# A hybrid attention trunk: the softmax denominators' small transfers issued by ScalarE instead of SyncE

## The chip, the cores and the metric

The kernel runs on one core of a Trainium2 chip. The metric is the device time of one execution in microseconds. Before the change it is 4072.53 us, the median of 3 runs (4071.81 to 4072.68).

## The reference

Two layers of a transformer trunk work on 1024 latent tokens and 256 context tokens of width 1024. Each layer has an input projection, four parallel mixers, an output projection and an MLP. Three of the mixers are attentions, and the kernel runs each as several heads:

```python
# A: neighbourhood attention (latents) or dense (context), 4 heads
p = jax.nn.softmax(jnp.concatenate([s_loc, s_ctx], axis=-1), axis=-1)
# B: differential attention, 4 heads with two softmaxes each
p1 = jax.nn.softmax(jnp.einsum('bqhd,bkhd->bhqk', a, k1) * scale, axis=-1)
p2 = jax.nn.softmax(jnp.einsum('bqhd,bkhd->bhqk', b, k2) * scale, axis=-1)
out = jnp.einsum('bhqk,bkhe->bqhe', p1 - lam * p2, v)
# D: banded attention with a sink logit, 4 heads
p = jax.nn.softmax(jnp.concatenate([s_loc, s_ctx, s_sink], axis=-1), axis=-1)
```

The fourth mixer is a Fourier transform over tokens and channels. Everything is float32.

## The kernel before

The kernel is written by hand, engine by engine, with semaphores. In the attention stage of each layer there are 16 heads, numbered v: 0 to 7 are the B heads (four heads, two softmaxes each), 8 to 11 the A heads, 12 to 15 the D heads. Each head has three chunks of query tokens (512, 512 and 256), and each chunk is a job. A job is made of key steps: 12, 12 and 2 for a B head, 10, 10 and 2 for an A head, 9, 9 and 2 for a D head, 376 in all for a layer. A key step is one block of 128 keys: TensorE makes the scores (`scores`, lines 2190 to 2193) in one of three PSUM banks, ScalarE takes the exponential into one of five `prob` buffers (line 1446), and two steps later TensorE multiplies by the values (`values`, line 2210). In A and D heads VectorE adds a bias or a mask to the scores first (`add_bias`, lines 1788 and 1791).

Between the key steps TensorE and VectorE make the row maxima of the next job. This is done in pieces (`piece`, lines 2162, 1757 and 1765), spread over the key steps by a planner (`SLOT_PIECES`). Two PSUM banks hold the pieces, so TensorE cannot make a piece before VectorE has reduced the one two before it. Each engine runs its own instructions in order; a wait at one of them holds all that stand behind it.

The value matrix has 64 columns of ones beside its 64 columns of values, so one half of the output holds the values' sum and the other half the softmax denominators. ScalarE copies both to `o_raw` (`take`, line 1477) two steps after a job's last key step. What follows for a head v happens during head v + 1:

1. `denominators_out` (line 1056): one row of `o_raw`, 1280 numbers, goes to DRAM (`s_den`).
2. `denominators_in` (line 1062): it comes back spread over 128 partitions (`den_c`).
3. `invert` (line 1795): VectorE takes the reciprocals in its slot at the end of the head's first job (`RECIP_AT`; step 11 in a B head, 9 in an A head, 8 in a D head). It waits there for `den_c`.
4. `reciprocals` (line 1066): SyncE stores `den_r` to DRAM (`s_rden`), waits for it, and loads it back broadcast over 64 partitions (`rden`).
5. `scale` (line 1222): GpSimd multiplies `o_raw` by `rden`.
6. For odd heads of A and D, ScalarE and VectorE split the result in two parts (`upper_pair`, line 1465; `lower_pair`, line 1812) at the steps of `PAIR_AT`: the last step of the second job and the two steps after it. SyncE stores them (`store_out`, line 1077).

All transfers of the stage are issued by SyncE, in this order for each v (lines 1093 to 1127): the loads of head v + 1 (`load_head`, gated on the start of head v), in heads 9 and 10 eight loads of bias tables (`load_bias`), then `denominators_out(v - 1)`, `load_values(v + 1)`, `denominators_in(v - 1)`, at v = 1 the first bias tables, `reciprocals(v - 1)`, at v = 8 the Fourier stage's loads, at v = 12 and 13 the transform matrices (`load_transform`), and the stores of a finished pair. ScalarE issues transfers only in the stage before (lines 1332 and 1407).

Of the kernel before, what the change touches and what calls it, by code (L numbers as in the profile page):

```python
# [23 lines left out]
P = 128  # L24
# [4 lines left out]
TOK = LAT + SEQ  # L29
# [10 lines left out]
NCH = len(CHUNKS)  # L40
# [88 lines left out]
def attention_jobs():  # L129

    jobs, v = [], 0
    for kind, heads in (("B", [(h, s) for h in range(4) for s in range(2)]), ("A", [(h, 0) for h in range(4)]),
                        ("D", [(h, 0) for h in range(4)])):
        for h, s in heads:
            for c in range(NCH):
                jobs.append((kind, h, s, c, v))
            v += 1
    return jobs
# [48 lines left out]
JOBS = attention_jobs()  # L187
NJ = len(JOBS)
# [14 lines left out]
NV = NJ // NCH  # L203
# [37 lines left out]
TAKE_AT = [STEP0[j + 1] + LAG for j in range(NJ)]  # L241
# [148 lines left out]

RECIP_AT = [STEP0[(v + 1) * NCH + 1] - 1 for v in range(NV - 1)]
assert len(set(ROW_AT)) == NJ and len(set(TAKE_AT)) == NJ
PAIR_AT = {STEP0[(v + 1) * NCH + 2] - 1 + c: (v, c) for v in PAIRS if v < NV - 1 for c in range(NCH)}
D_JOBS = [j for j in range(NJ) if JOBS[j][0] == "D"]
T_USES = [sum(1 for i in range(NT) if i % 2 == b) for b in range(2)]
# [29 lines left out]
def trunk(nc, I, O):  # L425
# [4 lines left out]
    def sem(name):  # L430
        return ctx.enter_context(nc.semaphore(name))
# [10 lines left out]
    def at(name, shape, dt, off):  # L442
        size = 4 * int(np.prod(shape[1:]))
        assert off + size <= top, (name, off + size, top)
        return nc.alloc_sbuf_tensor_at(name, shape, dt, offset=off).ap(), off + size

    def put(name, shape, dt=F32):
        ap, cur["c"] = at(name, shape, dt, cur["c"])
        cur["c"] = -(-cur["c"] // 32) * 32
        return ap  # L450
# [5 lines left out]
    for s in range(3):  # L456
        a, o = at(f"w_hi{s}", [P, 2048], F32R, W0 + s * 16384)
# [68 lines left out]
    a, o = at("w_hi3", [P, 2048], F32R, TMP2 + 8192)  # L526
# [63 lines left out]
    fc_r, o = at("fc_r", [P, FKT, 256], F32, cur["c"])  # L590
    flip, o = at("flip", [P, P], F32, o)
# [5 lines left out]
    o_raw = [put(f"o_raw{i}", [P, TOK]) for i in range(2)]  # L597
    rden = put("rden", [P, TOK])
    den_c, den_1, den_r = put("den_c", [P, TOK // P]), put("den_1", [P, TOK // P]), put("den_r", [P, TOK // P])
# [11 lines left out]
    def scratch(name, shape):  # L611
        return nc.dram_tensor(name, shape, F32).ap()
# [5 lines left out]
    s_den, s_rden = scratch("s_den", [16, TOK]), scratch("s_rden", [16, TOK])  # L618
# [43 lines left out]
    sink_p, o_mul, o_free = sem("sink_p"), sem("o_mul"), sem("o_free")  # L662
    den_out, den_in, den_rdy, rden_out, rden_in = (sem("den_out"), sem("den_in"), sem("den_rdy"), sem("rden_out"),
                                                   sem("rden_in"))
# [15 lines left out]
    def settle(e):  # L680

        e.sem_inc(seen, 1)  # L682
# [169 lines left out]
    def _(sp):  # L852
# [30 lines left out]
        for l in range(DEPTH):  # L883
# [116 lines left out]
            def load_transform(x):  # L1000
                sp.dma_start(dft_t[:, x], I["k_dft_lat"][x].rearrange("(t p) n -> p t n", p=P)).then_inc(f_in, 16)
                sp.dma_start(dft_x[:, x], I["k_dft_ctx"][x].rearrange("(t p) n -> p t n", p=P)).then_inc(f_in, 16)
# [44 lines left out]
            def load_bias(h):  # L1047

                for w, tab, sm in ((0, na_q[h % 2], bq_in[h % 2]), (1, na_k[h % 2], bk_in[h % 2])):
                    for half, c0, r, n in BIAS_PARTS[w]:  # L1050
                        sp.dma_start(tab[half * 64:half * 64 + 64, c0:c0 + n * GRID_W],
                                     s_toe[l, h, w, :, r * GRID_W:(r + n) * GRID_W]).then_inc(sm, 16)
# [3 lines left out]
            def denominators_out(v):  # L1056
                h = JOBS[v * NCH][1]
                d = 64 - 64 * (h % 2)
                sp.wait_ge(o_free, l * NJ + (v + 1) * NCH)
                sp.dma_start(s_den[v:v + 1], o_raw[v % 2][d:d + 1]).then_inc(den_out, 16)  # L1060

            def denominators_in(v):
                sp.wait_ge(den_out, l * NV * 16 + (v + 1) * 16)
                sp.dma_start(den_c, s_den[v].rearrange("(p t) -> p t", p=P)).then_inc(den_in, 16)

            def reciprocals(v):
                h = JOBS[v * NCH][1]
                o = 64 * (h % 2)
                sp.wait_ge(den_rdy, l * NV + v + 1)
                sp.dma_start(s_rden[v].rearrange("(p t) -> p t", p=P), den_r).then_inc(rden_out, 16)  # L1070
                sp.wait_ge(rden_out, l * NV * 16 + (v + 1) * 16)
                if v:
                    sp.wait_ge(o_mul, l * NV + v)
                sp.dma_start(rden[o:o + 64], bass.AP(tensor=s_rden.tensor, offset=v * TOK, ap=[[0, 64], [1, TOK]])
                             ).then_inc(rden_in, 16)
# [17 lines left out]
            for v in range(NV):  # L1093
                kind, h = JOBS[v * NCH][:2]
                if v + 1 < NV:
                    load_head(v + 1)
                if kind == "A" and 1 <= h < 3:
                    sp.wait_ge(s1_max, l * PIECES + PIECE0[v * NCH])
                    settle(sp)
                    sp.wait_ge(s2_add, l * NADD + ADD0[v * NCH])  # L1100
                    load_bias(h + 1)
                if v:
                    denominators_out(v - 1)
                if v + 1 < NV:
                    load_values(v + 1)
                if v:
                    denominators_in(v - 1)
                if v == 1:
                    sp.wait_ge(toe_in, (l + 1) * TOE_DMAS * 16)
                    sp.wait_ge(b_init, l * 4 + 4)  # L1110
                    settle(sp)
                    load_bias(0)
                    load_bias(1)
                if v:
                    reciprocals(v - 1)
                if kind == "A" and h == 0:
                    load_fourier()
                if v * NCH == FIRST_D:
                    sp.wait_ge(s1_max, l * PIECES + PIECE0[FIRST_D])
                    settle(sp)  # L1120
                    sp.wait_ge(s2_add, l * NADD + ADD0[FIRST_D])
                    settle(sp)
                if kind == "D" and h < 2:
                    load_transform(h)
                if v - 1 in PAIRS:
                    for cc in range(NCH):
                        store_out(JOBS[(v - 1) * NCH][0], JOBS[(v - 1) * NCH][1] // 2, cc)
# [189 lines left out]
    def _(act):  # L1317
# [36 lines left out]
        for l in range(DEPTH):  # L1354
# [70 lines left out]
            def max_row(j):  # L1425

                kind, _, _, c, v = JOBS[j]
                c0, n = CHUNKS[c]
                r, dst = (96, q1[v % 2]) if kind == "B" else (64, q2[v % 2])
                act.wait_ge(m_rowp, l * NJ + j + 1)  # L1430
                act.activation(dst[r:r + 1, c0:c0 + n], bank[r:r + 1, 7, :n], ACT.Copy, scale=-1.0).then_inc(m_rdy, 1)  # L1431
# [33 lines left out]
            def upper_pair(v, c):  # L1465
                c0, n = CHUNKS[c]
                act.wait_ge(o_mul, l * NV + v + 1)
                upper_out(pair_index(v, c), o_ad[:, c0:c0 + n], n)

            def take(j):  # L1470

                c0, n = CHUNKS[JOBS[j][3]]
                v = JOBS[j][4]
                act.wait_ge(pv_done, l * STEPS + STEP0[j + 1])
                if v >= 2:
                    act.wait_ge(o_mul, l * NV + v - 1)
                act.activation(o_raw[v % 2][:, c0:c0 + n], bank[:, 5 + j % 2, :n], ACT.Copy).then_inc(o_free, 1)

            max_row(0)
            for s in range(STEPS + LAG + 1):  # L1480
                if s < STEPS:
                    j, i = STEP_JOB[s]
                    exponentials(j, i)
                if s in ROW_AT:
                    max_row(ROW_AT.index(s))
                if s < STEPS and i == 0 and JOBS[j][0] == "D":
                    sink_row(j)
                if s in TAKE_AT:
                    take(TAKE_AT.index(s))
                if s in PAIR_AT:  # L1490
                    upper_pair(*PAIR_AT[s])

# [109 lines left out]
    def _(dve):  # L1602
# [33 lines left out]
        for l in range(DEPTH):  # L1636
# [175 lines left out]
            def lower_pair(v, c):  # L1812
                c0, n = CHUNKS[c]
                lower_out(pair_index(v, c), o_ad[:, c0:c0 + n], n)
# [5 lines left out]
            for s in range(STEPS + LAG + 1):  # L1820
# [7 lines left out]
                if s in RECIP_AT:  # L1828
                    invert(RECIP_AT.index(s))
                if s - 1 in PAIR_AT:  # L1830
                    lower_pair(*PAIR_AT[s - 1])

# [575 lines left out]
```

## Time and profile before

| what | value |
|---|---|
| median of 3 runs | 4072.53 us |
| profiled execution, its own time | 4076.61 us |
| its span, first to last instruction | 4074.9 us |
| mean granted TensorE clock | 0.977 |
| TensorE busy | 3845.0 us (94%) |
| VectorE busy | 2099.4 us (52%) |
| ScalarE busy | 916.3 us (22%) |
| GpSimd busy | 558.4 us (14%) |

The engine names in the rows are PE (TensorE matmul), PEld (its weight load), DVE (VectorE), ACT (ScalarE), POOL (GpSimd) and SPq and ACTq (the issuing of transfers by SyncE and ScalarE). An engine is busy from the start to the end of an instruction; the brackets at the end of a line tell how long it stood idle before, and what ended the wait. A transfer has two times: that of its issue, which holds the issuing engine, and that to its landing, which is told apart.

### The profile page before, as it was taken

Reading aid. Unit: us, or ns where it says so; the run is one execution under the profiler, and the core shown is the slowest. Engines: PE = TensorE matmul, PEld = TensorE weight load, DVE = VectorE, ACT = ScalarE, POOL = GpSimd, SP = SyncE. Lnnn points to the kernel's source line nnn. Section 1 sums busy time; section 2 is a strip of 40 time slices with the busy share of each in tenths; the row PEclk is TensorE's granted clock in tenths of the full one; section 3 lists DMA queues with packets and bytes.
Section 4 is the critical chain, followed back from the end, with each engine's and each line's share of the span. In section 5 each row is a group of like instructions: output and inputs, shape, how many; then the busy total and the mean of one; then the engine's idle time right before and its main releaser. Section 6 shows DMA issues by size and latency. Waiting matters only on the chain. (4 is left out here: it accounts for less than half of the span.)

```text
span 4074.9 us, 47294 instructions
## 1 busy us (share of the span) xinstructions
PE 3845.0 (94%) x18444; PEld 2989.6 (73%) x18444; DVE 2099.4 (52%) x3442; ACT 916.3 (22%) x1718; POOL 558.4 (14%) x432
## 2 busy tenths in 40 slices
PE   6898999889999999999989989999999999999998
PEld 4787556565888888888868855566568888888886
DVE  5222555555476666665572245555546545454445
ACT  3111455443210000000031125544512000000002
POOL 0011011101211111111131101110022111111112
PEclk8999999999999999999999989999999999999999
DMA  6754223564122122112215433256440100110011
GB/s 228 224 186 127 65 54 80 140 144 145 43 83 63 47 73 73 54 56 73 63 51 183 137 82 83 50 125 138 106 166 32 42 32 32 42 42 32 32 42 52
DMA packets 289646, 358.53 MB, mean 88 GB/s; under 512 B 102994, under 2 KB 215508, under 8 KB 289296
## 3 DMA queue, kind: packets, MB, share of 16 engines
q1 hardware_dynamic: 269008, 350.54, 29.5%
q10 hardware_dynamic: 20416, 4.98, 0.6%
q8 instruction: 146, 2.39, 0.2%
q14 instruction: 76, 0.62, 0.1%
HBM read 288.28 MB, written 72.16 MB: 88 GB/s over the span
## 5 line engine op out<-in xcount | busy, mean ns | idle before, releaser
L2056 PE MATMUL bank<-h_hi,w_hi 128*128 128x512 f32 (+1 forms) x2496 | 905.4, 363 | 21.1 <-issue 14.7
L2057 PE MATMUL bank<-h_lo,w_hi 128*128 128x512 f32 (+1 forms) x2496 | 886.2, 355 | 0.0
L2058 PE MATMUL bank<-h_hi,w_lo 128*128 128x512 f32 (+1 forms) x2496 | 886.0, 355 | 0.0
L2210 PE MATMUL bank<-prob,vv 128*128 128x512 f32 (+3 forms) x1504 | 703.7, 549 | 0.0
L1874 DVE SCALAR_TENSOR_TENSOR xT<-bank,mods,xT 128x512 f32<-128x512 f32 (+1 forms) x816 | 536.8, 661 | 321.9 <-PE bank L2058 305.2
L2056 PE MATMUL bank<-m_hi,w_hi 128*128 128x512 f32 (+1 forms) x1536 | 569.8, 371 | 53.1 <-DVE xT L1874 51.3
L2056 PEld LDWEIGHTS bank<-h_hi,w_hi 128*128 128x128 f32 x2496 | 472.7, 189 | 103.5 <-issue 33.8
L2058 PE MATMUL bank<-m_hi,w_lo 128*128 128x512 f32 (+1 forms) x1536 | 547.0, 356 | 0.0
L2057 PE MATMUL bank<-m_lo,w_hi 128*128 128x512 f32 (+1 forms) x1536 | 546.0, 355 | 0.0
L2057 PEld LDWEIGHTS bank<-h_lo,w_hi 128*128 128x128 f32 x2496 | 472.8, 189 | 73.4 <-issue 7.7
L2058 PEld LDWEIGHTS bank<-h_hi,w_lo 128*128 128x128 f32 x2496 | 472.6, 189 | 66.7
L1757 DVE TENSOR_REDUCE mp<-bank 128x1 f32<-128x512 f32 (+1 forms) x576 | 378.0, 660 | 274.1 <-PE bank L2162 273.3
L1557 ACT ACTIVATE m_r<-bank 128x512 f32<-128x512 f32 (+1 forms) x192 | 100.9, 527 | 1676.6 <-PE bank L2058 1676.6
L1446 ACT ACTIVATE prob<-bank 128x512 f32<-128x512 f32 (+1 forms) x576 | 329.0, 573 | 387.9 <-PE bank L2190 264.1
L2056 PEld LDWEIGHTS bank<-m_hi,w_hi 128*128 128x128 f32 x1536 | 289.7, 189 | 136.0 <-DVE xT L1874 87.1
L2162 PE MATMUL bank<-k,q 96*128 96x512 f32 (+4 forms) x768 | 288.4, 391 | 78.3 <-DMA sink_rows<-in_k_sink_rows 30.7
L1914 DVE TENSOR_TENSOR m_f<-m_r 128x512 f32<-128x512 f32 (+1 forms) x192 | 115.6, 603 | 461.6 <-ACT m_r L1557 461.6
L2190 PE MATMUL bank<-q,k 97*128 97x512 f32 (+1 forms) x416 | 322.5, 775 | 1.8 <-ACT q L1431 1.8
L2058 PEld LDWEIGHTS bank<-m_hi,w_lo 128*128 128x128 f32 x1536 | 290.0, 189 | 43.1
L2057 PEld LDWEIGHTS bank<-m_lo,w_hi 128*128 128x128 f32 x1536 | 290.5, 189 | 41.4 <-issue 0.9
L715 POOL TENSOR_SCALAR w_hi<-stage 128x2048 fp32r<-128x2048 f32 x90 | 173.5, 1927 | 1073.6 <-issue 537.1
L719 DVE TENSOR_TENSOR w_lo<-stage,w_hi 128x2048 fp32r<-128x2048 f32 x90 | 212.8, 2364 | 186.4 <-POOL w_hi L715 186.4
(187 smaller groups left out, 4080.7 us busy)
## 6 DMA issues: line engine op xcount, KB each, us to landing
stage<-in_w_mlp SPq DMA_DIRECT2D x64, 1024.0 KB, 5.2
nx_w<-in_w_ada SPq DMA_DIRECT2D x16, 1536.0 KB, 9.2
stage<-in_w_in SPq DMA_DIRECT2D x18, 1024.0 KB, 6.3
ada_h<-in_w_ada SPq DMA_DIRECT2D x16, 1024.0 KB, 7.9
rope_t<-in_k_rope SPq DMA_DIRECT2D x28, 512.0 KB, 4.4
k<-s_kB SPq DMA_DIRECT2D x48, 224.0 KB
k<-s_kA SPq DMA_DIRECT2D x24, 448.0 KB, 10.5
k<-s_kD SPq DMA_DIRECT2D x24, 448.0 KB, 10.7
```

What stands on the lines that cost most here:

```text
L715: pool.tensor_scalar(w_hi[slot], stage, 1.0, 0.0, ALU.mult, ALU.add).then_inc(whi_rdy, 1)
L719: dve.tensor_tensor(w_lo[slot], stage, w_hi[slot].bitcast(F32), ALU.subtract).then_inc(wlo_rdy, 1)
L1446: act.activation(prob[si % NP_RING][:, :n], src, ACT.Exp, scale=FS if kind == "B" else 1.0).then_inc(p_rdy, 1)
L1757: dve.tensor_reduce(mp[j % 2][:, t, x:x + 1], src, AX.X, ALU.max).then_inc(s1_max, 1)
L1874: dve.scalar_tensor_tensor(out=x, in0=bank[:, bk, :n], scalar=mods[l][:, gate + k, cd:cd + 1], in1=x, op0=ALU.mult, op1=ALU.add).then_inc( ...
L1914: dve.tensor_tensor(m_f[m][:, :n], m_r[m][:, :n], m_r[m][:, :n], ALU.mult).then_inc(sqr_rdy, 1)
L2056: x = pe.matmul(out, a_hi, b_hi, start=first, stop=False)
L2057: pe.matmul(out, a_hi, b_lo, start=False, stop=False)
L2058: return x, pe.matmul(out, a_lo, b_hi, start=False, stop=last)
L2162: pe.matmul(bank[:, gi % 2, :n], q1[v % 2][0:rows, q0:q0 + P], k1[v % 2][0:rows, key0:key0 + n], start=True, stop=True).then_inc(s1_full, 1)
L2190: mm = pe.matmul(out, k1[b][0:97, k], q1[b][0:97, q], start=True, stop=True)
L2210: pe.matmul(ob[:, q0:q0 + n], vv[h % 2][:, key0 // P], prob[si % NP_RING][:, :n], start=(i == 0 and kind != "D"), stop=(i == len(steps) - ...
```

## The change

The four transfers of a head's denominators leave SyncE's order and are issued by ScalarE at fixed key steps of the next head. Counted from the first step of head v + 1, the transfer out comes after step 3, the one in after step 7 (B) or 6 (A and D), the reciprocals' store two steps after VectorE's slot, and their broadcast load six (B) or five steps after it (the kind is that of head v). Only the last head of each layer keeps SyncE's versions.

```diff
+DEN_OUT_AT = {TAKE_AT[(v + 1) * NCH - 1] + 1: v for v in range(NV - 1)}
+DEN_IN_AT = {s + (4 if JOBS[v * NCH][0] == "B" else 3): v for s, v in DEN_OUT_AT.items()}
+RDEN_OUT_AT = {s + 2: v for v, s in enumerate(RECIP_AT)}
+RDEN_IN_AT = {s + 6 if JOBS[v * NCH][0] == "B" else s + 5: v for v, s in enumerate(RECIP_AT)}
...
-                if v:
-                    denominators_out(v - 1)
                 if v + 1 < NV:
                     load_values(v + 1)
-                if v:
-                    denominators_in(v - 1)
...
-                if v:
-                    reciprocals(v - 1)
...
+            def denominators_out(v):
+                d = 64 - 64 * (JOBS[v * NCH][1] % 2)
+                act.wait_ge(o_free, l * NJ + (v + 1) * NCH)
+                act.dma_start(s_den[v:v + 1], o_raw[v % 2][d:d + 1]).then_inc(den_out, 16)
+
+            def denominators_in(v):
+                act.wait_ge(den_out, l * NV * 16 + (v + 1) * 16)
+                act.dma_start(den_c, s_den[v].rearrange("(p t) -> p t", p=P)).then_inc(den_in, 16)
+
+            def reciprocals_out(v):
+                act.wait_ge(den_rdy, l * NV + v + 1)
+                act.dma_start(s_rden[v].rearrange("(p t) -> p t", p=P), den_r).then_inc(rden_out, 16)
+
+            def reciprocals_in(v):
+                o = 64 * (JOBS[v * NCH][1] % 2)
+                act.wait_ge(rden_out, l * NV * 16 + (v + 1) * 16)
+                if v:
+                    act.wait_ge(o_mul, l * NV + v)
+                act.dma_start(rden[o:o + 64], bass.AP(tensor=s_rden.tensor, offset=v * TOK, ap=[[0, 64], [1, TOK]])
+                              ).then_inc(rden_in, 16)
...
+                if s in DEN_OUT_AT:
+                    denominators_out(DEN_OUT_AT[s])
+                if s in DEN_IN_AT:
+                    denominators_in(DEN_IN_AT[s])
+                if s in RDEN_OUT_AT:
+                    reciprocals_out(RDEN_OUT_AT[s])
+                if s in RDEN_IN_AT:
+                    reciprocals_in(RDEN_IN_AT[s])
                 if s in PAIR_AT:
                     upper_pair(*PAIR_AT[s])
```

## Rows read from the trace of the kernel before

**Rows 1.** The page, part 1: busy time, share of the span and instructions.

```profile
PE 3845.0 (94%) x18444; PEld 2989.6 (73%) x18444; DVE 2099.4 (52%) x3442; ACT 916.3 (22%) x1718; POOL 558.4 (14%) x432
```

**Rows 2.** Waits, longest in total: total us, times, longest us.

```profile
DVE den_r L1801 <- DMA den_c<-s_den: 58.6, 12, 6.7
```

**Rows 3.** Stretches (heads 8, 9, 11, 13): us; PE, PEld, DVE, ACT, POOL; clock, DMA, GB/s.

```profile
692.80:723.00 30.20, 29.94 (x124) 20.11 (x124) 20.05 (x65) 14.59 (x28) 5.83 (x2) 1.00 0.69 164
723.00:762.00 39.00, 32.87 (x126) 22.09 (x125) 20.23 (x66) 14.58 (x28) 2.89 (x1) 0.91 0.54 119
...
800.00:833.00 33.00, 29.96 (x123) 20.03 (x122) 20.38 (x63) 15.63 (x31) 2.92 (x1) 1.00 0.57 137
...
863.00:896.00 33.00, 27.63 (x107) 18.47 (x106) 14.91 (x42) 13.76 (x28) 2.90 (x1) 0.90 0.68 168
```

**Rows 4.** Timeline of head 9: start us, us, what, idle before and its releaser.

```profile
723.08 0.45 SPq L1023 DMA_DIRECT2D q<-s_qA  x1
...
732.70 0.44 SPq L1060 DMA_DIRECT2D s_den<-o_raw  x1
...
733.60 4.20 SPq L1042 DMA_DIRECT2D vv<-in_cache_na_v  x1
...
741.97 0.34 SPq L1064 DMA_DIRECT2D den_c<-s_den  x1
744.52 0.22 DVE L1801 RECIPROCAL den_r<-den_c 128x10 f32<-128x10 f32 x1 [6.63 <-DMA den_c<-s_den]
...
745.30 0.80 PE L2162 MATMUL bank<-k,q 128*128 128x512 f32 x1 [5.88 <-DVE mp L1765]
```

**Rows 5.** Timeline of head 9, ScalarE's exponentials of steps 3 and 6.

```profile
728.40 0.60 ACT L1446 ACTIVATE prob<-bank 128x512 f32<-128x512 f32 x1 [0.57 <-PE bank L2193]
...
734.03 0.63 ACT L1446 ACTIVATE prob<-sb 128x512 f32<-128x512 f32 x1 [1.21 <-DVE sb L1791]
```

**Rows 6.** Timeline of heads 8, 12 and 13: inversions, a head's start, a piece.

```profile
708.13 0.22 DVE L1803 RECIPROCAL den<-den_c 128x10 f32<-128x10 f32 x1 [0.46 <-DMA den_c<-s_den]
...
833.08 0.44 SPq L1023 DMA_DIRECT2D q<-s_qD  x1
...
849.10 0.22 DVE L1801 RECIPROCAL den_r<-den_c 128x10 f32<-128x10 f32 x1 [3.04 <-DMA den_c<-s_den]
...
881.24 0.22 DVE L1801 RECIPROCAL den_r<-den_c 128x10 f32<-128x10 f32 x1 [4.76 <-DMA den_c<-s_den]
...
882.06 0.79 PE L2162 MATMUL bank<-k,q 128*128 128x512 f32 x1 [3.11 <-DVE mp L1757]
```

**Rows 7.** Two stretches, columns as in rows 3 (DMA share is next to last).

```profile
729.00:735.00 6.00, 6.00 (x26) 3.99 (x24) 4.95 (x17) 1.81 (x4) 0.00 (x0) 1.00 1.01 216
272.80:278.80 6.00, 6.00 (x52) 6.00 (x51) 0.00 (x0) 0.35 (x1) 1.45 (x1) 1.00 0.97 313
```

**Rows 8.** Line 1332 (ScalarE's queue), the one transfer issued at 213.44.

```profile
DMA to landing us min/median/max: 2.2/2.2/2.2
```

**Rows 9.** Line 1332, the one transfer issued at 272.77.

```profile
DMA to landing us min/median/max: 6.0/6.0/6.0
```

**Rows 10.** Line 1064, the loads of `den_c`, all 32.

```profile
DMA to landing us min/median/max: 1.5/2.1/2.8
```

**Rows 11.** Line 1051, the `na_q` table loads of head 9.

```profile
L1051 SPq DMA_DIRECT2D na_q<-s_toe x4: 597/597/1317, 726.9 to 729.5; - x4
...
DMA to landing us min/median/max: 9.7/10.2/10.8
```

**Rows 12.** Line 1074, the broadcast loads of `rden`, all 32.

```profile
DMA to landing us min/median/max: 3.5/3.8/4.3
```

**Rows 13.** Timeline of head 12, GpSimd's multiplication.

```profile
855.16 2.92 POOL L1234 TENSOR_TENSOR o_ad<-o_raw,rden 64x1280 f32<-64x1280 f32 x1 [26.16 <-DMA rden<-s_rden]
```

**Rows 14.** Timeline before attention, an issue of SyncE.

```profile
204.65 1.44 SPq L953 DMA_DIRECT2D cache_n<-in_cache_na_k  x1
```

**Rows 15.** Timeline before attention, an issue of ScalarE.

```profile
205.38 0.83 ACTq L1332 DMA_DIRECT2D s_toe<-in_na_rpb_rev  x1
```

## The prediction

> **What bounds the kernel now.** I read the engine totals first: TensorE is busy for 94% of the span, ScalarE for 22% [rows 1]. A change that only moves DMA issues can gain only where TensorE stands still or runs at a lower clock. Then the waits: VectorE waited 58.6 us, in 12 waits of up to 6.7 us, for `den_c`, the denominators on their way back from DRAM [rows 2]. Then busy time in stretches of one attention head each (v counts the 16 heads of a layer: 0 to 7 are B, 8 to 11 A, 12 to 15 D). Head 8 takes 30.2 us and TensorE is busy for 29.94 of them at full clock. Head 9, with the same work, takes 39.0: TensorE is busy for 32.87 us at a mean clock of 0.91. Head 13 takes 33.0 at 0.90 [rows 3]. So the reader should see some 9 us lost in one head: about 6 in idle time and 2.9 in matmuls at the lower level (1.2 against 2.4 GHz) right after it.
>
> The timeline of head 9 shows who does it [rows 4]. SyncE starts the next head's loads at 723.08, issues the tiny `s_den` store only at 732.70, behind 14 large loads, spends 4.20 us on issuing one `vv` load from 733.60, and can issue the `den_c` load only at 741.97. VectorE, whose slot for the inversion came at 737.89 (744.52 - 6.63), starts it at 744.52, and TensorE, whose next row piece needs VectorE, has stood for 5.88 us at 745.30. Head 11 has 33.0 - 29.96 = 3.0 us of idle time at full clock, against 0.3 in head 8 [rows 3]. In head 12 VectorE waits 3.04, in head 13 4.76, and TensorE then stands for 3.11 [rows 6]. So TensorE's idle time is the wait less 0.75 in A and less 1.65 in D, which makes 1.4 for head 12. In head 8 VectorE waits 0.46. The B heads do not wait at all: the 12 waits lie in heads 9 to 14 of the two layers.
>
> **The change, part by part.** Removed from SyncE: for 15 of 16 heads in each layer two waits with the transfers out and in, and the two waits around the reciprocals. Its next items then start earlier: the Fourier loads of head 8, the transform loads of heads 12 and 13. They are no nearer to their use, so I count nothing for them, except that they keep the DMA engines full while the small transfers run. Behind every later head load SyncE is held by its own gates, which stay.
>
> Added to ScalarE: four issues for each of these 30 heads. I take SyncE's 0.44 us of 732.70 for each, 1.8 a head, 53 us in all. ScalarE waited 0.57 and 1.21 us before the two steps shown [rows 5], with two steps of score banks ahead of it. An issue of 0.44 fits, so I count 0; without that cover it would be 53 us.
>
> Moved: the first transfer now leaves after key step 3. In head 9 that exponential starts at 728.40 and takes 0.60, so the transfer goes at 729.0, which is 6.0 after the head's start and 3.7 earlier than now. The second goes after step 6, 734.03 + 0.63 = 734.66, so 11.6 after the start at the earliest [rows 5]. What decides is how long a transfer takes to land on ScalarE's queue while SyncE's queue fills the DMA engines: their share was 1.01 between 729 and 735 [rows 7]. The trace of before has no such denominators, only ScalarE's table writes. One issued at 213.44 into idle engines landed in 2.2 us, one at 272.77 with a share of 0.97 in 6.0 [rows 8, 9, 7]: 3.8 more. `den_c` itself lands in 1.5 us at best [rows 10]. The bounds are therefore 1.5 (no delay) and 10.8, the slowest table load in SyncE's own queue [rows 11]. I take 1.5 + 3.8 = 5.3 for both, because the write at 272.77 is the nearest row: small pieces, same queue, full engines. Then `s_den` has landed at 6.2 + 5.3 = 11.5, just before step 6 asks, and `den_c` at 11.7 + 0.34 + 5.3 = 17.3 after the head's start. The slot comes at 14.8 in an A head (737.89 - 723.08) and at 13.0 in a D head (849.10 - 3.04 - 833.08) [rows 4, 6]: waits of 2.5 and 4.3 remain.
>
> The Trainium skill (DMA: Bandwidth & Descriptors, Queues, rings and completion order) says that each DMA engine alternates between the queues at packet granularity. By that rule a transfer of one packet would hardly be delayed and the sum would be that of the first rival; the 3.8 us above speak against taking it whole.
>
> What comes next in heads 9 and 10: the first piece after the inversion needs the bias table of the next head. Its last `na_q` load is issued at 729.5 and lands 10.2 us later, at 739.7 [rows 11], 16.6 after the head's start. That is the next wait, and it is just inside 17.3.
>
> The sum for the first layer, in TensorE time:
> - Heads 9 and 10: idle 5.88 becomes 2.5 - 0.75 = 1.75, so -4.1, and the slow matmuls go, -2.9 (32.87 - 29.94): head 11 had more idle time than that at a clock of 1.00. -7.0 each, -14.0.
> - Head 8: a wait of 0.46 becomes 2.5: +1.6.
> - Head 11: 3.0 becomes the 0.3 of head 8, -2.7; its pieces leave VectorE more room, so a wait of 2.5 hides.
> - Head 12: 3.04 becomes 4.3: +1.3.
> - Head 13: its store stood behind the output stores and goes early now, so I take half of 4.76 (-2.4) and half of the clock loss of 3.3 (33.0 x 0.10), -1.7: -4.1. Its wait for the next head's `k`, which comes before, stays.
> - Head 14: even.
> - Cost at the pairs: the broadcast back is issued five steps after the inversion instead of right behind the reciprocals, lands in 3.8 [rows 12], and GpSimd multiplies for 2.92 [rows 13]. ScalarE's `upper_pair` asks four steps later in D, some 5.5 us (30.2 / 22 x 4), against 0.44 + 3.8 + 2.92 = 7.2: ScalarE waits 1.7 in heads 12 and 14, of which I count 1 each for TensorE, and 1.3 for the head load queued behind the pair's stores on SyncE: +3.3. Nothing (slack covers it) and 5 are the ends.
>
> Together -14.6. The second layer repeats the pattern with slightly shorter waits; I count -12. In all -26.6: 4050.0 against the 4076.61 of the profiled execution (span 4074.9), which lies 4.1 above the median of 4072.53. Against that median it is 4046.
>
> **Rivals.**
 Then the bias table is the limit in heads 9 and 10 (1.8 late; -4.8 and -2.9 each), head 11 gives 2.7, head 12 1.4, head 13 3.1 + 3.3, head 14 as head 12; less 3.3: -24.0 and some -17 in the second layer, 4032. For it: the transfers are tiny. Against it: rows 8 and 9.
> 2. *The delay enters twice and is larger.* The place is ScalarE's wait at step 6 and then VectorE's inversion; the head loads have longer rows than anything that ran at 272.77. At 6.1 us each `den_c` comes at 6.2 + 6.1 + 0.34 + 6.1 = 18.7. Heads 9 and 10 keep 3.2 of idle time (-3.7 each with part of the clock), head 11 gives 2.0; heads 8, 12 and 14, which hardly waited, lose 3.1, 2.7 and 2.7 and half of a clock loss of 2.9 each (4.4); pairs and ScalarE's own wait 4.3: +7.8, with the second layer +14, 4087: slower. It decides from about 5.9 us. At 9.3, the most that `s_den` can have taken on SyncE's queue (732.70 to 741.97), it would be far worse.
> 3. *ScalarE's issue is held while SyncE issues.* Step 6 of head 9 comes at 734.66, inside the 4.20 us issue of 733.60 that ends at 737.80 [rows 4]. Held until then, `den_c` is 3.1 later in heads 9 and 10 and the clock falls again: 4 x 6 back, -2.6 in all, 4070. Against it: an issue of ScalarE at 205.38, 0.73 into one of 1.44 on SyncE, took its usual 0.83 [rows 14, 15]. The Trainium skill (Perfetto Trace Analysis, DMA Instruction, HWDGE) has the descriptor generator locked for one issuer at a time, which would give this rival; those two rows do not show it.
>
> **How the numbers follow.** The forecast has 0.52, rival 1 0.23, rival 2 0.17, rival 3 0.08. The first two are faster by over 0.2% (8 us, about what a measurement of this kernel tells from no change): 0.75; rival 3 is within it, 0.08; rival 2 slower, 0.17. The range reaches below rival 1 by its unknown pair cost (3.3 for each layer), to 4026, and up to near rival 2, 4084; beyond lie the worse half of rival 2 and little else. The likeliest case alone spans 4032 to 4060 (landings of 4.5 to 5.6, pair cost 0 to 10).
>
> **What would show it.** Right: `den_c` leaves on ScalarE's queue some 12 us after a head's start and lands in 4.5 to 6 us; heads 9 and 10 last about 32 us at a clock of 1.00; VectorE still waits 2 to 4 us there and now also in head 8; SyncE has no line for `den_c` except for the last head; ScalarE waits 1 to 2 us for `o_ad` at the pairs. The step on the landing is wrong if VectorE's total wait for `den_c` falls below 10 us (rival 1) or rises above 60 (rival 2); the step on ScalarE is wrong if its issues take over 1 us or B heads grow longer. The prediction fails if heads 9 and 10 stay at 38 to 39 us.

## The result, and the profile after

The changed kernel is slower: 4093.7 us, median of 6 runs (4086.18 to 4094.96), against 4072.17 for the kernel before in the same rounds (4070.27 to 4073.48). The ratio is 1.0051, with a 95% interval of 1.0039 to 1.0063, so +21.5 us where 26.6 less were forecast. The profiled execution took 4094.96 us.

The engine totals on the changed kernel's page and then its waits, longest in total (total us, times, longest us), which answer to [rows 1, 2]:

```profile
span 4093.3 us, 47294 instructions
...
PE 3858.1 (94%) x18444; PEld 2995.1 (73%) x18444; DVE 2111.7 (52%) x3442; ACT 916.0 (22%) x1718; POOL 557.3 (14%) x432
```

```profile
DVE den_r L1828 <- DMA den_c<-s_den: 55.6, 12, 6.5
...
ACT prob L1444 <- DVE den_r L1828: 18.0, 6, 3.5
...
ACT prob L1444 <- DMA s_den<-o_raw: 13.5, 6, 2.6
...
DVE den L1830 <- DMA den_c<-s_den: 6.8, 2, 3.6
```

The wait that the change was aimed at is no smaller (58.6 + 1.1 us before, 55.6 + 6.8 now), and ScalarE has two waits that it did not have: 18.0 us for VectorE's reciprocals, which are late because VectorE waits, and 13.5 us for the first transfer. The first number to look at next is therefore not a total but where the waits moved to.

A head's time below is the distance between the last evacuations of `o_raw` (line 1475) of two successive heads; in brackets VectorE's wait for `den_c` in that head, all of it in the first layer:

| us | head 8 | 9 | 10 | 11 | 12 | 13 | 14 |
|---|---|---|---|---|---|---|---|
| before | 30.2 (0.5) | 39.0 (6.6) | 38.3 (6.4) | 32.8 (6.2) | 28.0 (3.0) | 34.9 (4.8) | 27.9 (3.0) |
| after | 35.0 (3.6) | 37.6 (4.9) | 38.0 (5.0) | 31.4 (4.9) | 35.3 (6.2) | 33.6 (4.8) | 28.8 (2.5) |

The B heads have not changed (34.32 us both). Heads 9, 10, 11 and 13 gain 1.4, 0.3, 1.3 and 1.3 us; heads 8 and 12 lose 4.8 and 7.2. The second layer gives the same picture: head 8 goes from 30.4 to 36.1 and head 12 from 27.8 to 35.3, and nothing else moves by more than 1.3. So the loss sits in exactly the two places in front of which SyncE's queue has large loads that now start early: the Fourier loads (head 8) and the transform loads (head 12; head 13 has such loads too and does not lose).

The timeline of head 8 after the change (start us, us, what, idle before and its releaser; compare [rows 6]):

```profile
698.70 0.24 ACTq L1480 DMA_DIRECT2D s_den<-o_raw  x1
...
701.17 2.34 SPq L993 DMA_DIRECT2D fc_n<-s_v  x1
...
703.55 2.88 SPq L994 DMA_DIRECT2D fc_r<-s_v  x1
...
706.47 0.34 ACTq L1484 DMA_DIRECT2D den_c<-s_den  x1
...
706.88 4.11 SPq L996 DMA_DIRECT2D fc_r<-s_v  x1
...
711.81 0.22 DVE L1830 RECIPROCAL den<-den_c 128x10 f32<-128x10 f32 x1 [3.64 <-DMA den_c<-s_den]
...
712.84 0.50 PE L2189 MATMUL bank<-k,q 128*128 128x512 f32 x1 [3.14 <-DVE mp L1792]
```

Each issue is cheap (0.24 and 0.34 us), but it takes 7.8 us from the issue of `s_den` until the next transfer can be issued and `den_c` lands 5.3 us after its own issue, while SyncE's issues of the Fourier loads stretch to 2.3 to 4.1 us each. In head 12 the same happens with the transform loads (lines 1005 and 1006):

```profile
841.57 0.24 ACTq L1480 DMA_DIRECT2D s_den<-o_raw  x1
...
843.18 3.03 SPq L1005 DMA_DIRECT2D dft_t<-in_k_dft_lat  x1
...
846.25 2.24 SPq L1006 DMA_DIRECT2D dft_x<-in_k_dft_ctx  x1
...
848.80 0.34 ACTq L1484 DMA_DIRECT2D den_c<-s_den  x1
849.25 0.68 ACT L1444 ACTIVATE prob<-sb 128x256 f32<-128x256 f32 x2 [2.10 <-DMA s_den<-o_raw]
...
854.53 0.22 DVE L1828 RECIPROCAL den_r<-den_c 128x10 f32<-128x10 f32 x1 [6.22 <-DMA den_c<-s_den]
...
855.35 0.80 PE L2189 MATMUL bank<-k,q 128*128 128x512 f32 x1 [3.60 <-DVE mp L1784]
```

And what the stall costs on TensorE, in stretches (us; PE, PEld, DVE, ACT, POOL; clock, DMA share, GB/s): head 8, head 9, head 12, and then 7 us each before, in and behind the stall of head 12:

```profile
693.30:728.30 35.00, 31.60 (x124) 20.92 (x124) 20.05 (x65) 14.59 (x28) 3.82 (x2) 0.95 0.61 141
728.30:766.10 37.80, 33.29 (x127) 22.37 (x126) 20.18 (x66) 14.55 (x29) 4.93 (x2) 0.91 0.56 122
...
835.30:872.50 37.20, 32.08 (x125) 21.85 (x125) 19.95 (x49) 16.48 (x34) 2.90 (x1) 0.91 0.53 126
...
842.00:849.00 7.00, 7.00 (x32) 4.70 (x31) 4.67 (x16) 2.20 (x5) 0.00 (x0) 1.00 1.07 207
849.00:856.00 7.00, 2.68 (x11) 2.01 (x12) 1.24 (x4) 3.39 (x7) 0.00 (x0) 0.87 0.68 206
856.00:863.00 7.00, 7.00 (x16) 3.62 (x15) 2.23 (x5) 1.20 (x3) 0.00 (x0) 0.64 0.00 0
```

Read the last three together. The DMA engines are full (1.07) while `s_den` is under way; TensorE then works for 2.68 of 7 us; and behind the stall it is busy all the time, but at a granted clock of 0.64 (most of the 7 us at the lower level); the trace has 16 matmul records there against 32 before the stall. Head 8, which ran at 1.00 before [rows 3], now runs at 0.95, and head 9 is still at 0.91: TensorE stood for 4.13 us there, and the clock came down. VectorE's wait alone does not say so. In head 11 it is as long (4.88 us), but TensorE stands for only 1.34 us and the clock stays at 1.00:

```profile
749.23 0.79 PE L2189 MATMUL bank<-k,q 128*128 128x512 f32 x1 [4.13 <-DVE mp L1792]
...
822.72 0.22 DVE L1828 RECIPROCAL den_r<-den_c 128x10 f32<-128x10 f32 x1 [4.88 <-DMA den_c<-s_den]
823.37 0.74 PE L2189 MATMUL bank<-k,q 128*128 128x256 f32 x2 [1.34 <-DVE mp L1784]
...
806.10:837.50 31.40, 29.71 (x120) 19.78 (x119) 19.42 (x62) 14.31 (x28) 2.92 (x1) 1.00 0.60 136
```

### The profile page after: what moved, and what is told of

It is laid out like the page before. It is cut to its first block and busy times, and to the rows that moved or that the text cites. A ratio compares the mean times of both kernels' runs of the same rounds, so it can differ in the third digit from the quotient of the medians.

```text
span 4093.3 us, 47294 instructions
## 1 busy us (share of the span) xinstructions
PE 3858.1 (94%) x18444; PEld 2995.1 (73%) x18444; DVE 2111.7 (52%) x3442; ACT 916.0 (22%) x1718; POOL 557.3 (14%) x432
## 5 line engine op out<-in xcount | busy, mean ns | idle before, releaser
L2237 PEld LDWEIGHTS bank<-prob,vv 128*128 128x128 f32 x1504 | 274.6, 195 | 55.2 <-ACT prob L1444 9.8
```

The source lines that it names most:

```text
L2237: pe.matmul(ob[:, q0:q0 + n], vv[h % 2][:, key0 // P], prob[si % NP_RING][:, :n], start=(i == 0 and kind != "D"), stop=(i == len(steps) - ...
```

## The experiments

Three theories stood when they began, under the names that the expectations use. T1: the two transfers, slow one after the other on ScalarE's queue because of the head loads that both kernels have, set VectorE's wait for `den_c`, and that wait with the lower clock behind it is the loss. T2: the loss comes from the Fourier and transform loads, which lost their hold in SyncE's queue and now fill the DMA engines while the small transfers run. T3: ScalarE's own waits in front of its exponentials set the time. A second question was whether the place of VectorE's inversion, and not the transfers' queue, was the loss in the kernel before. What a run gains or loses in us against the kernel before is worked out from its ratio.

**e1_late_loads.** The changed kernel, with SyncE held until VectorE has made the reciprocals before it issues the two groups of loads. (In the kernel before they stood behind the reciprocals' two transfers as well.)

```diff
                 if kind == "A" and h == 0:
+                    sp.wait_ge(den_rdy, l * NV + v)
                     load_fourier()
...
                 if kind == "D" and h < 2:
+                    sp.wait_ge(den_rdy, l * NV + v)
                     load_transform(h)
```

> The changed kernel with one edit: SyncE waits for the previous head's inversion before it issues the Fourier loads (head 8) and the transform loads (heads 12, 13), as it did before the change. Theory T1 (two landings in series on ScalarE's queue, 7.2 and 5.3 us, are slow because of the head loads, which both kernels have): heads 8 and 12 stay near 35.0 and 37.2 us, 4088 to 4094. Theory T2 (the loads that moved earlier keep the DMA engines full and are the extra cost): head 8 falls from 35.0 to about 32, head 12 from 37.2 to 31 to 33, head 13 a little, 8 us a layer, 4078.

Measured: 4069.96 us, ratio 0.9998 (0.9989 to 1.0007). Heads 8 and 12 are back at 30.6 and 28.7 us. The whole loss is gone, and nothing is gained. That is T2's direction and more than its size (4078 was expected); T1, by which nothing would have changed, is out as the account of the 22 us. The timeline of head 8 of this kernel:

```profile
700.46 0.24 ACTq L1482 DMA_DIRECT2D s_den<-o_raw  x1
...
708.20 0.34 ACTq L1486 DMA_DIRECT2D den_c<-s_den  x1
...
710.81 0.22 DVE L1832 RECIPROCAL den<-den_c 128x10 f32<-128x10 f32 x1 [0.88 <-DMA den_c<-s_den]
711.33 0.36 SPq L993 DMA_DIRECT2D fc_n<-s_v  x1
```

Two things are to be seen. `den_c` lands 2.6 us after its issue instead of 5.3, with the Fourier loads behind it, at 711.33; in head 12 the inversion follows its issue by 1.9 us instead of 5.7. And `s_den` still takes 7.7 us: that part has nothing to do with the moved loads. It is the next head's own loads, as g3 will show.

**f3_fourier_late_only.** Of e1's two waits, only the first.

> The changed kernel with only the Fourier loads late; the transform loads stay early. T2, separable: head 8 near 30.6 us as in e1, head 12 near 35.3 as in the changed kernel; 4080 to 4085.

Measured: 4079.26 us, 1.0026 (1.0016 to 1.0036), halfway between the changed kernel and e1. Head 8 is at 30.7 us again and head 12 stays at 35.0. The two groups of loads cost about 10 and 11 us and add up. (The time is just under the 4080 that was expected.)

**f1_before_early_loads.** The converse on the kernel before: both groups of loads placed ahead of the `den_c` load in SyncE's queue, with the waits that guard those of head 12, and with the transfers left where they were.

```diff
                     load_values(v + 1)
+                if kind == "A" and h == 0:
+                    load_fourier()
...
+                if kind == "D" and h < 2:
+                    load_transform(h)
                 if v:
                     denominators_in(v - 1)
```

> The kernel before (all transfers on SyncE) with one edit: the Fourier loads of head 8 and the transform loads of heads 12 and 13 are issued before the load of den_c instead of after the reciprocals. T2 (these loads, in front of or beside the denominators' transfers, are the loss, whichever queue carries them): heads 8 and 12 grow by 5 to 9 us each in both layers, head 13 by 0 to 4; 4090 to 4105. Rival (they hurt only through ScalarE's queue, where the transfers wait twice): within 3 us of before.

Measured: 4112.6 us, 1.0108 (1.0094 to 1.0122), 44 us worse than before and beyond what was expected. In head 8 the load waits for its turn in the queue and VectorE waits 10.30 us:

```profile
705.78 3.95 SPq L992 DMA_DIRECT2D fc_r<-s_v  x1
...
712.45 0.43 SPq L1064 DMA_DIRECT2D den_c<-s_den  x1
...
717.68 0.22 DVE L1803 RECIPROCAL den<-den_c 128x10 f32<-128x10 f32 x1 [10.30 <-DMA den_c<-s_den]
```

So with loads that start early, a queue of their own spared the small transfers about half of the harm (22 us instead of 44). That is what the change bought, against a harm that the kernel before did not have.

**e3_den_in_2_later.** ScalarE issues the `den_c` load two key steps later from head 7 on, so that it never stands waiting for `s_den`.

```diff
-DEN_IN_AT = {s + (4 if JOBS[v * NCH][0] == "B" else 3): v
+DEN_IN_AT = {s + (4 if v < 7 else 5): v
```

> The changed kernel with den_c's load two key steps later in heads 8 to 14 (steps 8 instead of 6), so that ScalarE does not wait for s_den. T1 (what sets the time is when den_c arrives at VectorE): den_c arrives 0.7 us or so later, 4094 to 4106. T3 (ScalarE's 2 us waits in front of its exponentials set the time, VectorE's are side by side with them): 4075 to 4088.

Measured: 4092.02 us, 1.0056 (1.0043 to 1.0070), not to be told from the changed kernel, and between the two ranges that were expected. ScalarE's own waits for `s_den` fall from 13.5 to 1.1 us and nothing is gained. The run is not clean, as VectorE's waits in heads 9 to 11 grow by 0.5 to 0.6, to 5.4 and 5.5 us; but T3's 6 us or more are not there. Beside VectorE's longer wait, ScalarE's 13.5 us cost nothing that can be seen.

**e2_before_slot_later.** Now the other question. The kernel before, its transfers untouched, with VectorE's slot for the inversion moved later by 1 to 5 key steps.

```diff
-RECIP_AT = [STEP0[(v + 1) * NCH + 1] - 1 for v in range(NV - 1)]
+LATER = {7: 1, 8: 5, 9: 5, 10: 5, 11: 2, 12: 4, 13: 2}
+RECIP_AT = [STEP0[(v + 1) * NCH + 1] - 1 + LATER.get(v, 0) for v in range(NV - 1)]
```

> The kernel before (all transfers on SyncE) with VectorE's inversion 1, 5, 5, 5, 2, 4, 2 key steps later in heads 8 to 14, so that it comes after den_c has landed. T1 (VectorE's wait for den_c and the lower clock behind it are the whole loss): heads 9 and 10 fall from 39.0 and 38.0 to 31 or 32 us at a clock of 1.00, head 13 to 29 or 30, VectorE's wait from 58.6 to under 10 us, 4025 to 4035. Rival (another wait takes its place: the bias table that lands 16.6 us after the head's start, or ScalarE at the pairs): heads 9 and 10 at 34 or more, 4050 to 4070.

Measured: 4028.01 us, 0.9894 (0.9879 to 0.9910), 43 us faster, as T1's sentence on VectorE's wait had it for this kernel. Heads 8 to 14 take 30.0, 31.0, 31.7, 29.7, 26.4, 27.9 and 26.4 us. Nothing was made earlier: `den_c` still leaves SyncE's queue at 742.48 in head 9, and the inversion at 745.29 no longer waits for it. That settles what the 58.6 us of [rows 2] were: a slot too early, more than a transfer too late. The waits that are left in this kernel:

```profile
DVE junk L1766 <- DMA na_q<-s_toe: 6.6, 3, 2.3
...
PE bank L2163 <- DMA k<-s_kD: 4.2, 3, 2.5
...
DVE den_r L1802 <- DMA den_c<-s_den: 2.3, 4, 1.0
```

The bias table is next, as the prediction's working on `na_q` had it.

**e4_after_slot_later.** The changed kernel with later slots as well (2 to 4 steps), and with the broadcast back at 1 and 3 steps behind the inversion instead of 2 and 5.

> The changed kernel with VectorE's inversion 2 to 4 key steps later in heads 8 to 14, the reciprocals' store one step after it and the broadcast three steps after it. T1 with VectorE's wait as the place of the loss: its wait for den_c falls from 55.6 to under 10 us, heads 8, 9, 10 and 12 lose 3 to 6 us each, ScalarE waits 2 to 4 us at the pairs; 4045 to 4060. T3 (ScalarE's wait for s_den and the pairs is as dear): 4070 to 4085, with heads 9 and 10 still at 35 us or more.

Measured: 4041.76 us, 0.9937 (0.9924 to 0.9951). Most of e2's gain, though not all, and a little better than expected: ScalarE now waits 14.8 us for `o_ad` at the pairs and 13.2 us for `s_den`. The Fourier and transform loads still start early here, and yet head 8 takes 30.8 us (30.2 in the kernel before): what the Fourier loads cost the changed kernel, they cost through a slot that asks early.

**f2_late_loads_slot_later.** e1 with e2's slots, so both repairs and the transfers on ScalarE, with the broadcast at its 5 steps.

> The changed kernel with the loads late again (as e1) and VectorE's inversion 1, 5, 5, 5, 2, 4, 2 key steps later in heads 8 to 14 (as e2); the broadcast stays five steps behind the inversion. If the queue does not matter once nobody waits for den_c: as e2, 4026 to 4032. Rival (ScalarE's waits for s_den at step 6 of 1.5 to 2 us and for o_ad at the pairs stay and cost): heads 10, 12 and 14, which hold pairs, 2 to 4 us longer than in e2, 4040 to 4055.

Measured: 4066.33 us, 0.9995 (0.9986 to 1.0004): no gain, the surprise of the series, and beyond both ranges that were expected. VectorE no longer waits for `den_c`; heads 10, 12 and 14 take 39.9, 32.3 and 32.8 us. These are the heads with a pair of finished heads to write. The timeline shows the chain at the first pair:

```profile
778.56 0.33 ACTq L1491 DMA_DIRECT2D s_rden<-den_r  x1
...
782.58 0.46 ACTq L1498 DMA_DIRECT2D rden<-s_rden  x1
...
789.52 0.63 ACT L1464 ACTIVATE ao_hi<-o_ad 128x512 fp32r<-128x512 f32 x1 [5.92 <-POOL o_ad L1235]
...
791.34 0.64 PE L2192 MATMUL bank<-k,q 128*128 128x320 f32 x1 [5.34 <-DVE mp L1795]
```

The broadcast leaves 4 us after the reciprocals, as its step in ScalarE's stream says, and not the moment they have landed. GpSimd's product comes late, ScalarE waits 5.92 us for it with the exponentials queued behind, and TensorE stands for 5.34. Such waits at the pairs make 29.0 us in this kernel. The wait for `den_c` had only changed its place.

**g1_prompt_broadcast.** f2 with the broadcast issued 1 and 2 steps behind the inversion.

```diff
-RDEN_OUT_AT = {s + 2: v for
+RDEN_OUT_AT = {s + (1 if v > 6 else 2): v for
-RDEN_IN_AT = {s + 6 if JOBS[v * NCH][0] == "B" else s + 5: v
+RDEN_IN_AT = {s + (2 if v > 6 else 6): v
```

> f2 with the reciprocals' store one step behind VectorE's inversion and the broadcast one step behind that, in heads 8 to 14 (f2: two and five). If ScalarE's waits for o_ad at the pairs (29.0 us in 6 waits in f2) are what f2 loses against e2: they fall to under 10 us, heads 10, 12 and 14 from 39.9, 32.3 and 32.8 to within 1 or 2 us of e2's 31.7, 26.4 and 26.4; 4028 to 4036. If ScalarE's waits for s_den at step 6 count too: 4038 to 4048.

Measured: 4050.19 us, 0.9951 (0.9939 to 0.9964), 16 better than f2 and 22 short of e2, just outside what was expected. The waits of ScalarE:

```profile
ACT prob L1447 <- DMA s_rden<-den_r: 10.6, 4, 4.0
...
ACT prob L1447 <- DMA s_den<-o_raw: 8.0, 4, 2.2
ACT ao_hi L1464 <- POOL o_ad L1235: 7.5, 4, 2.1
```

With slots so close, ScalarE itself now waits for the transfers to land, and its exponentials stand behind them. Issued late, the broadcast delays the pairs; issued promptly, it stops ScalarE. SyncE, with nothing of the inner loop in its stream, has no such choice to make. 22 us lie between this kernel and e2, whose `den_c` slots are the same. They are not the least that the new place of the transfers can cost: e4, with other slots, the broadcast three steps behind the inversion and the loads not even held, came to 4041.76, 14 us from e2.

**f4_hold_values.** e1, with SyncE held in front of the next head's large `vv` loads until `den_c` has landed.

```diff
+                if 8 <= v < NV - 1:
+                    sp.wait_ge(den_in, l * NV * 16 + v * 16)
                 if v + 1 < NV:
                     load_values(v + 1)
```

> e1 with the next head's value loads (about 0.45 MB) also held on SyncE until den_c has landed, in heads 8 to 14. If the landing on ScalarE's queue depends on what SyncE has in flight at that moment: den_c lands in 2 to 3 us instead of up to 7 in heads 9 to 13, VectorE's waits there fall from 4.5 to 1 to 3 us, 4045 to 4065. If the 2.3 MB head loads and the tables decide and the values hardly count: waits as in e1, 4066 to 4074, or worse where the values then come late.

Measured: 4051.16 us, 0.9957 (0.9943 to 0.9971). That is 19 us better than e1, over half of it in head 13, which falls from 33.9 to 29.2 us in this layer and from 33.6 to 28.3 in the other, with waits of 1.9 and 3.0; head 12 takes 30.3 instead of 28.7. In heads 9, 10 and 11 `den_c` still lands in 5.9 to 6.5 us, where 2 to 3 were expected, and the waits are 4.2, 4.0 and 3.1: what stands ahead of `vv` is still under way there, the bias tables in heads 9 and 10 (in head 9 the last of them lands at 740.52 and `den_c` at 740.35) and the `q` and `k` loads in head 11. And in head 8 it still takes 7.3 us from the issue of `s_den` (696.29) to that of `den_c` (703.61).

**g3_s_den_ahead.** So the changed kernel once more, with SyncE held before a head's loads until `s_den` of the head before has landed.

```diff
                 if v >= 2:
                     sp.wait_ge(s2_full, l * STEPS + STEP0[(v - 1) * NCH])
+                if v >= 9:
+                    sp.wait_ge(den_out, l * NV * 16 + (v - 1) * 16)
```

> The changed kernel with SyncE's loads for the next head held until s_den has landed, in heads 8 to 14: not meant to be fast. If s_den's 7.2 to 7.8 us on ScalarE's queue are a wait behind the head loads that SyncE has just issued: it lands in under 2.5 us now, so that the load of den_c is issued at step 6 without a wait, while den_c itself, now beside the late head loads, stays slow; the next head's k and tables come late and the time is 4100 to 4160. If the landing is slow for another reason (the single descriptor, ScalarE's queue itself): 6 us or more again.

Measured in one run: 4128.41 us, against 4069.62 for the kernel before. As a change it is a bad one, since every head's `k` is now late:

```profile
PE bank L2191 <- DMA k<-s_kD: 31.1, 6, 5.4
```

And the collision has only moved: `den_c`, now issued beside the head's loads, lands in 8.3 to 10.8 us, and VectorE waits 55.9 + 11.2 us for it.

As a measurement it is clear: ScalarE never waits for `s_den` any more (there is no such line), and the distance to the next issue falls to what the key steps dictate, 6.6, 5.6 and 4.5 us in heads 8, 9 and 12 instead of 7.8, 7.5 and 7.2. The DMA queues show it directly (packets, MB, share of 16 engines; q1 is SyncE's queue, q10 ScalarE's). In the changed kernel's head 9, `s_den` is issued at 733.74. From then to 739.6 only SyncE's queue moves data, and the one packet of `s_den` starts in the 0.6 us after that (first two stretches, 733.74 to 739.6 and 739.6 to 740.2). In g3 it is issued at 733.19 and is through within 1 us (last line, 733.19 to 734.19):

```profile
DMA packets 252, 1.29 MB, mean 219 GB/s; under 512 B 47, under 2 KB 47, under 8 KB 252
q1 hardware_dynamic: 252, 1.29, 103.1%
...
q1 hardware_dynamic: 26, 0.10, 81.3%
q10 hardware_dynamic: 1, 0.01, 4.3%
...
q10 hardware_dynamic: 2, 0.01, 1.3%
```

The 4.3% of 16 engines in 0.6 us are 0.41 us. So of the 7.5 us until the next issue some 5.9 are a wait of `s_den` before it moves at all, and 0.4 its own transfer. That wait is due to the head's loads on SyncE's queue, which a queue of its own does not get it past.

**g2_e2_tables_first.** The version that the runs pointed to: e2, with the second halves of an A or D head's `q` and `k` moved behind the bias tables, and slots of heads 12 and 14 one step later (LATER 11: 3, 13: 3).

```diff
-                    sp.dma_start(q2[b][0:64].bitcast(F32), ...)
-                    sp.dma_start(k2[b][0:64].bitcast(F32), ...)
...
                 S, vb = rest_in[v % 2], h % 2
+                if kind != "B":
+                    sp.dma_start(q2[b][0:64].bitcast(F32), ...)
+                    sp.dma_start(k2[b][0:64].bitcast(F32), ...)
```

> e2 with the inversion one step later still in heads 12 and 14 and the q2 and k2 loads of the next A or D head issued after its bias tables, just before the value loads. If what is left in heads 9 and 10 of e2 is the wait for the na_q table (6.6 us in 3 waits): it vanishes, 4020 to 4026. Rival (the pairs or the next k take it over): 4026 to 4034.

Measured: 4019.88 us, 0.9873 (0.9858 to 0.9888): 52 us faster than the kernel before and 1.8% faster than the changed one, the best of all, though its interval still touches that of e2. Stretches of heads 9 and 13 (columns as above):

```profile
727.50:757.50 30.00, 29.74 (x126) 20.26 (x124) 20.21 (x66) 14.55 (x29) 2.92 (x1) 1.00 0.71 153
846.80:874.50 27.70, 26.40 (x116) 18.88 (x114) 15.34 (x44) 14.35 (x30) 2.91 (x1) 1.00 0.83 189
```

Head 9 takes 30.0 us at full clock where it took 39.0 at 0.91 [rows 3]. The wait for `na_q` is gone; what is left is 3.2 us for `k` in the D heads.

## Why the prediction was wrong

**The step that failed** is the sentence on what is removed from SyncE: "They are no nearer to their use, so I count nothing for them, except that they keep the DMA engines full". It looked at the loads as work with a deadline and not as traffic with a start. What counts is not when the Fourier and transform loads are needed but that they had been standing behind the reciprocals, by the order of SyncE's queue alone, and so could never run beside `den_c`. Measured, that step is worth 22 us (e1), about half for each group (f3). Without it the change would have been within 0.2% of the kernel before. Of the 48 us between forecast and result it explains these 22; the other 26, all that the change was to gain, are left to the second step and to the smaller parts below.

**The second step** is the size of the landings. The prediction took 5.3 us for both, the best `den_c` landing and the 3.8 us between two table writes of line 1332. Measured, `s_den` took 7.2 to 7.9 us until `den_c` was issued, in heads 8 to 14 without head 11 (5.6), and `den_c` took 5.3 to 7.8 in heads 8 to 13. That it was the transfer and not the key step is seen in ScalarE's waits of up to 2.6 us in the D heads, and in head 8 by the distance from the start of the exponential just before the issue: 1.2 us, against 0.1 in g3. Its two ends, 1.5 and 10.8, did hold them. In head 9 `den_c` left 12.9 us after the head's first load (728.39) and landed 20.0 after it, against 17.3 in the working, and the wait was 4.9 instead of 2.5. The -7.0 for each of heads 9 and 10 became -1.4 and -0.3, as TensorE still stood for over 4 us there and the clock still came down; the prediction had both the idle time and the clock loss vanish together. By its own mark ("fails if heads 9 and 10 stay at 38 to 39 us") they as good as did, at 37.6 and 38.0.

**The others, by its parts.** Four issues on ScalarE at no cost: right, they take 0.23 to 0.55 us and the B heads did not change. Head 8 +1.6: +4.8, through the Fourier loads. Head 11 -2.7: -1.3. Head 12 +1.3: +7.2, through the transform loads. Head 13 -4.1: -1.3. Head 14 even: +0.9. The cost at the pairs had the right place and mechanism, ScalarE's wait for `o_ad` behind a broadcast five steps late. In the changed kernel itself it is small (four waits with 4.7 us together, where 1.7 each were taken), but in f2 it is 29.0, and a prompt broadcast (g1) gave back 16 of the 38 us that f2 lacks against e2.

**The rivals.** Rival 2 had the direction and almost the time (4087 against 4093.7): the transfers' delay enters twice, that of `s_den` is over its threshold of 5.9 us, and heads 8 and 12 lose. It was right on VectorE's inversion; of the other place, ScalarE's wait at step 6, no cost can be seen in this kernel (e3); and it did not name the moved loads, without which e1 comes out even. So its number is partly luck. Rival 1, no queueing, is excluded by the landings of heads 8 to 13 and by the 5.9 us in which `s_den` did not move. It had been worked out from the Trainium skill (DMA: Bandwidth & Descriptors, Queues, rings and completion order), which has each DMA engine take turns between the queues packet by packet. That a lone small transfer would slip through was the prediction's own step: the same sentence of the page lets an engine drain a whole packet, typically some 9 to 17 descriptors, before it switches. The profile's packets are taken here for single descriptors. The 205 of them over 512 bytes between 733.74 and 739.6 filled 103.1% of 16 engines for 5.86 us, so about 0.47 us each, and 9 to 17 of them would make 4.2 to 8.0 us: an estimate, from the page's numbers of descriptors and the two lines under g3. The 5.9 us lie inside it, so these runs do not speak against the page; that it was this that held `s_den` back is not shown. Rival 3, an issue held while SyncE issues, did not happen: at 741.25, inside SyncE's issue of 4.34 us from 738.68, the issue on ScalarE took its usual 0.34:

```profile
738.68 4.34 SPq L1046 DMA_DIRECT2D vv<-in_cache_na_v  x1
...
741.25 0.34 ACTq L1484 DMA_DIRECT2D den_c<-s_den  x1
```

**What the prediction did not ask.** It read [rows 2, 4] as a transfer that comes too late. The same rows say as well that the consumer asks too early: what is made of the reciprocals is asked for only at the steps of a pair. Moving VectorE's slot gave 43 us (e2) with the queues untouched.

**What stays open.** Why `s_den` waits 5.9 us behind loads on another queue before it moves (the order inside the DMA engines) was not tested, only that it does and that the loads are the reason. Nor is the difference of 22 us between e2 and g1 split between ScalarE's in-order waits and the late head loads that follow from late pairs, although both show in its trace: 9 us of it lie in head 13 of the two layers, where TensorE waits 2.17 us for `k` and later 2.68 for ScalarE in the first. And with later slots no run compares early and held loads with all else equal: e4, with early ones, is 8 us faster than g1, with held ones, but has other slots and another broadcast, and the two intervals just overlap.

## What to carry to other kernels

Before taking a wait out of an in-order queue, list what stands behind it and ask beside what each item will now run: the wait may be the only thing that keeps a large load away from a small transfer that somebody is waiting for. When an engine waits for a transfer inside its own fixed order, first see whether the slot that asks can come later, which costs a line or two and here gave twice what the change lost; another queue did not get the small transfers past DMA engines that were full. And be slow to let an engine with the inner loop's work in its stream wait for landings: issued late the transfer delayed its users (f2), issued promptly it stopped the loop (g1), and the best step between (e4) was still 14 us behind SyncE (e2).

## What the runs showed of the hardware

- A transfer of 5 KB on ScalarE's queue held the next one back for 7.2 to 7.9 us in most heads from 8 on, behind the loads on SyncE's (DMA share 1.07 in the stretch shown). In head 9 it did not begin to move for 5.9 of them and then took 0.41; with no loads beside it, it was through within 1 us (g3). The `den_c` load landed in 5.3 to 7.8 us; the fastest of the changed kernel took 1.5. The direction had been expected, the size had not.
- The same early loads cost 44 us when the small transfers stood in their queue (f1) and 22 when they stood in another (the change). The second queue halved this harm; it did not remove it.
- Single issues of SyncE stretched to 2.3 to 4.3 us while the engines were full, but an issue of ScalarE inside one of these took 0.34 us. What held SyncE's issue back did not hold the other queue's.
- Behind a stall of 3.6 us in head 12, TensorE was busy at a granted clock of 0.64 for 7 us. And in head 9, VectorE's wait fell from 6.6 to 4.9 us while the clock of the head stayed at 0.91: the shorter wait gave back most of its own length (the head 1.4 us) and none of what the clock costs. In head 11, where VectorE waited 4.9 us too and TensorE stood for 1.3, the clock stayed at 1.00.
